# A hybrid decoder step: expert loop reordered, normalisation sums in array groups, z projection threaded through the samples' state update

## The reference

```
h = rmsnorm(x, norm_mix_w) * (1 + sc1) + sh1
qkv, z, b, a, cq, ckv, kpe, gate_a, gate_b = split(h @ w_in)
# gated DeltaNet: 8 heads, DK = DV = 128
q, k = l2norm(q) * DK**-0.5, l2norm(k)                 # per head
# a sample's state S (8 samples x 8 heads x 128 x 128), one step:
S  = S * exp(g);  vn = beta * (v - k @ S);  S = S + outer(k, vn);  o = q @ S
o  = rmsnorm(o, gdn_norm_w) * silu(z)                  # per head, all tokens
# latent attention follows (cq, ckv, kpe ...), then the gates, w_out, and
# mixture of experts: top 4 of 32, for each expert e
gu = xb @ w_gu[e] + b_gu[e]                            # 1024 x 2048
gt, up = min(gu[:, :1024], 7), clip(gu[:, 1024:], -7, 7)
y  = ((up + 1) * gt * sigmoid(1.702 * gt)) @ w_dn[e] + b_dn[e]
out[token] += gate * y
```

## Time and profile before

| | us |
|---|---|
| median of 3 runs | 1761.97 (1761.94 to 1762.75) |
| profiled execution, its own time | 1762.21 |
| its span, first to last instruction | 1760.4 |

### The profile page before, as it was taken

The page is one execution under the profiler, slowest core; times in us unless marked ns, Lnnn a source line. Parts: engine busy times, 40 slices in busy tenths (PEclk is TensorE's granted clock), DMA queues, the critical chain, the costliest instruction groups (busy, mean ns, idle before and its releaser), DMA issues.

```text
span 1760.4 us, 25682 instructions
## 1 busy us (share of the span) xinstructions
PE 1630.7 (93%) x10122; PEld 892.3 (51%) x10122; DVE 495.6 (28%) x1067; ACT 319.1 (18%) x690; POOL 24.2 (1%) x18
## 2 busy tenths in 40 slices
PE   6999688799879999789999999999999999999996
PEld 4777676477547668533343434343433434343433
DVE  1555765511220102422212222222222122222223
ACT  2222121102221110211111211111111112111113
POOL 0000300000000000000000000000000000000000
PEclk8998899899979999879999999999999999999998
DMA  9638312434327986249999999999999999999990
GB/s 405 251 143 338 152 50 109 167 105 139 130 70 272 353 329 292 99 173 394 419 409 422 410 420 412 419 420 408 421 411 419 410 421 410 420 416 414 421 400 25
DMA packets 59535, 541.26 MB, mean 307 GB/s; under 512 B 7218, under 2 KB 11442, under 8 KB 28626
## 3 DMA queue, kind: packets, MB, share of 16 engines
q1 hardware_dynamic: 58754, 534.65, 74.9%
q0 software_dynamic: 720, 5.76, 0.8%
HBM read 533.54 MB, written 6.84 MB: 307 GB/s over the span
## 4 chain that ended last, share of the span: by engine, by line
PE 88%; DVE 7%; ACT 2%; DMA 1%; issue 1%; SPq 0%; POOL 0%; DVEq 0%; ACTq 0%
PE banks L507 25%; PE banks L548 13%; PE banks L1138 8%; PE banks L774 5%; PE banks L463 4%; PE banks L490 4%; PE banks L537 3%; PE banks L477 2%; PE banks L520 2%; PE banks L986 2%; PE banks L1011 2%; DMA ring<-wpre 1%; DVE regB L601 1%; PE banks L1036 1%; PE banks L727 1%; PE banks L872 1%
## 5 line engine op out<-in xcount | busy, mean ns | idle before, releaser
L507 PE MATMUL banks<-ring,regA 128*64 128x512 f32 x2048 | 454.5, 596 | 0.8 <-ACT regA L563 0.8
L507 PEld LDWEIGHTS banks<-ring,regA 128*64 128x64 f32 x2048 | 144.8, 137 | 287.5 <-issue 287.5
L548 PE MATMUL banks<-ring,regC 128*64 128x512 f32 x1024 | 226.8, 595 | 0.0
L601 DVE TENSOR_TENSOR regB<-regB,banks 128x528 f32<-128x528 f32 x132 | 87.0, 700 | 406.0 <-PE banks L490 406.0
L548 PEld LDWEIGHTS banks<-ring,regC 128*64 128x64 f32 x1024 | 70.7, 137 | 131.8 <-issue 127.9
L621 DVE TENSOR_SCALAR regA<-banks 128x512 f32<-128x512 f32 x32 | 22.1, 692 | 344.1 <-PE banks L520 344.1
L566 ACT ACTIVATE regA<-regA 128x512 f32<-128x512 f32 x32 | 20.1, 629 | 531.4 <-DVE regA L621 531.4
L463 PE MATMUL banks<-regC,regA 128*64 128x512 f32 (+1 forms) x396 | 99.7, 622 | 3.2 <-DVE regA L593 3.2
L490 PE MATMUL banks<-regA,regC 64*128 64x264 f32 x528 | 82.2, 422 | 12.6 <-DVE regB L601 11.9
L774 PE MATMUL banks<-hT,ring 128*128 128x264 f32 x384 | 90.3, 391 | 0.0
L774 PEld LDWEIGHTS banks<-hT,ring 128*128 128x128 f32 x384 | 71.5, 190 | 18.2 <-issue 6.8
(11 more groups left out here) (444 smaller groups left out, 1670.6 us busy)
## 6 DMA issues: line engine op xcount, KB each, us to landing
ring<-w_gu SPq DMA_DIRECT2D x128, 2048.0 KB, 10.6
ring<-w_dn SPq DMA_DIRECT2D x64, 2048.0 KB, 8.2
ring<-wpre SPq DMA_DIRECT2D x41, 2048.0 KB, 13.5
ring<-kvT SPq DMA_DIRECT2D x64, 256.0 KB, 4.6
ring<-kv SPq DMA_DIRECT2D x64, 256.0 KB, 6.3
ring<-ssm SPq DMA_DIRECT2D x2, 2048.0 KB, 10.7
o_ssms<-ring POOLq DMA_DIRECT2D x2, 2048.0 KB, 9.4
con_sb<-con SPq DMA_DIRECT2D x1, 1269.0 KB
```

Source lines behind the costliest of these rows:

```text
L507: mm = pe_mm(bank[x // 2][SLOT * (x % 2):SLOT * (x % 2 + 1), :], lhsT=hg[:, k % 4, SLOT * (k // 4):SLOT * (k // 4 + 1)], rhs=ring[c][:, 20 ...
L548: mm = pe_mm(bank[5][SLOT * y:SLOT * (y + 1), :], lhsT=actT[:, m % 4, SLOT * (m // 4):SLOT * (m // 4 + 1)], rhs=ring[c][:, D * (m % 4) + H ...
L601: V.tensor_tensor(pair, pair, banks[:, b:b + 2, 0:T], ALU.add).then_inc(acc_added, 1)
```

## The change

Three edits, made together.

1. **Expert loop.** The scatter's four steps use bank pairs 6-7, 2-3, 4-5, 6-7, and only step 3 waits, for addition 0. The turns of the activation come before the turn of the gathered tokens instead of after it (on ACT too), and the second pair of them waits for the copy of the gathered tokens out of bank 2. `act_` is written by DVE with its columns regrouped (each column 512 bytes from the one before), and the turns read 128 columns side by side.
2. **Row and column groups for the q/k norm and the output norm.** The sums of head i go to partitions 32 (i mod 4) on, with one-hot matrices of 4 (or 2) columns; root and reciprocal run over 128 partitions; the spreads take 4 (or 2) rows in the row group i mod 4. The decay's sums move from behind the 16 spreads to before spread 12.
3. **State update and z projection.** `krow` loses its zeros and each outer product runs over the 32 rows of its head. There are eight steps of two heads, into banks 0-1 and 2-3 in turn; DVE adds each in an operation of 1,024 elements per partition. `project_z` 0 runs before the first step, 1 and 2 are cut into quarters that stand between the eight steps, 3 and 4 follow the two state products, 5 the turns, 6 and 7 the norm's sums. They use banks 6 and 7 and keep all eight results in SBUF (`zs`). The eight spreads run in one go after projection 7, and DVE's multiplications of the heads with them.

```diff
+        SCATTER_BANKS = (6, 2, 4, 6)
...
-                    b = (6, 2)[q % 2]
-                    if q >= 2:
-                        pe.wait_ge(acc_added, j * 4 + q)
+                    b = SCATTER_BANKS[q]
+                    if q == 3:
+                        pe.wait_ge(acc_added, j * 4 + 2)
...
-                turn_gathered(j + 2)
                 pe.wait_ge(act_ready, j + 1)
                 for y in range(2):
+                    if y == 1:
+                        pe.wait_ge(gtok_copied, j + 2)
                     for q in (2 * y, 2 * y + 1):
-                        mm = pe_mm(bank[4 - 2 * y][:, P * q:P * (q + 1)], lhsT=act_[:, q::4], rhs=ident, start=True, stop=True)
+                        mm = pe_mm(bank[4 - 2 * y][:, P * q:P * (q + 1)], lhsT=act_[:, P * q:P * (q + 1)], rhs=ident, start=True, stop=True)
                     mm.then_inc(a_turned, 1)
+                turn_gathered(j + 2)
...
-                V.tensor_tensor(act_[:, :], upc[:, :], sgm[:, :], ALU.mult).then_inc(act_ready, 1)
+                V.tensor_tensor(act_[:, :].rearrange("p (q n) -> p n q", q=4), upc[:, :].rearrange("p (n q) -> p n q", q=4),
+                                sgm[:, :].rearrange("p (n q) -> p n q", q=4), ALU.mult).then_inc(act_ready, 1)
...
+            def group_sum(i, cols):
+                return bank[5][32 * (i % 4):32 * (i % 4) + 4, cols]
...
-                    pe_mm(bank[5][0:2 * H, 0:NPR], lhsT=row_sum(i), rhs=sqb[:, i % 2, 0:NPR], start=(i == 0), stop=(i == 2 * H - 1),
+                    pe_mm(group_sum(i, slice(0, NPR)), lhsT=row_sum(i // 4, 4), rhs=sqb[:, i % 2, 0:NPR], start=(i < 4), stop=(i >= 2 * H - 4),
...
+            def spread(i):
+                if i >= 4:
+                    pe.wait_ge(l2done, i - 3)
+                r = slice(32 * (i % 4), 32 * (i % 4) + 4)
+                pe_mm(bank[L2_BANKS[i % 4]][:, 0:T], lhsT=ident[r, 32 * (i % 4) + i // 4:32 * (i % 4) + i // 4 + 1].to_broadcast([4, P]),
+                      rhs=rsb[r, 0, :], start=True, stop=True).then_inc(l2ss, 1)
...
+                if i == 2 * H - 4:
+                    pe.wait_ge(bg_done, 1)
...
+                spread(i)
...
+            def project_z(m, first, last):
+                if first == 0:
+                    weights(pe, ZZ + m // 4)
+                    if m == 1:
+                        pe.wait_ge(stage("vnm_ready"), 1)
+                    if m >= 2:
+                        pe.wait_ge(stage("z_evac"), m - 1)
+                for k in range(first, last):
+                    mm = pe_mm(bank[7 - m % 2][:, 0:T], lhsT=chunk_k(ZZ + m // 4, m % 4, k), rhs=hT[:, k, :], start=(k == 0), stop=(k == KD - 1))
+                if last == KD:
+                    mm.then_inc(stage("z_ready"), 1)
+            def outer_product(g, x):
+                u = 4 * g + x
+                if x == 0:
+                    pe.wait_ge(stage("vnm_ready"), g + 1)
+                if u >= 2:
+                    pe.wait_ge(stage("snew"), u - 1)
+                for j in (2 * (x % 2), 2 * (x % 2) + 1):
+                    r = slice(32 * j, 32 * j + 32)
+                    mm = pe_mm(bank[j][:, :], lhsT=krow[r, g, :], rhs=vnm[r, g, 512 * (x // 2):512 * (x // 2) + 512], start=True, stop=True)
+                mm.then_inc(stage("outer"), 1)
+            project_z(0, 0, KD)
             pe.wait_ge(*once("krow_copied"))
             for g in range(2):
+                for x in range(4):
+                    outer_product(g, x)
+                    project_z(1 + g, 2 * x, 2 * x + 2)
             for g in range(2):
-                pe.wait_ge(stage("snew"), 3 + g)
-                mm = state_product(0, g, 2 * g)
+                pe.wait_ge(stage("snew"), 4 * g + 4)
+                state_product(0, g, 4 - 4 * g).then_inc(stage("oss_ready"), 1)
+                project_z(3 + g, 0, KD)
...
+            project_z(5, 0, KD)
             pe.wait_ge(stage("on_sq"), 1)
             for h in range(H):
+                mm = pe_mm(bank[3][32 * (h % 4):32 * (h % 4) + 2, 0:T], lhsT=row_sum(h // 4, 2), rhs=oM[:, h, :], start=(h < 4), stop=(h >= 4),
...
+            project_z(6, 0, KD)
+            project_z(7, 0, KD)
             pe.wait_ge(stage("on_root"), 1)
             for h in range(H):
+                if h >= 4:
+                    pe.wait_ge(stage("on_rs"), h - 3)
...
+            pe.wait_ge(stage("z_evac"), H)
...
+                if m % 4 == 2:
+                    pe.wait_ge(stage("on_rs"), H)
...
-            nc.gpsimd.memset(krow[:, :, :, :], 0.0).then_inc(once("krow_zero")[0], 1)
```

More of the change, by code:

```diff
@@ L273, in build_program @@
         stmp = cut(regC, 3700, NSA * P)
[L274 removed]
+        zs = cut(regC, 6600, H, T)
         rot = cut(regC, 8000, T)
@@ L570, in item @@
                 A(selT[:, :], bank[6][:, 0:T], ACT.Copy).then_inc(selT_copied, 1)
-                act.wait_ge(g_turned, j + 2)
-                A(hg[:, :, :], bank[3][:, :].rearrange("p (q s) -> p q s", q=4), ACT.Copy).then_inc(hg_ready, 1)
                 for y in range(2):
@@ L576, in item @@
                       ACT.Copy).then_inc(actT_ready, 1)
+                act.wait_ge(g_turned, j + 2)
+                A(hg[:, :, :], bank[3][:, :].rearrange("p (q s) -> p q s", q=4), ACT.Copy).then_inc(hg_ready, 1)
                 act.wait_ge(moe_read, j * 6 + 6)
@@ L810, in _ @@
-            pe.wait_ge(bg_done, 1)
-            for c in range(2):
-                pe_mm(bank[6][:, 64 + 16 * c:72 + 16 * c], lhsT=upto, rhs=g_tok[:, c, :], start=True, stop=True)
-                pe_mm(bank[6][:, 72 + 16 * c:80 + 16 * c], lhsT=ones, rhs=g_tok[:, c, :], start=True, stop=True)
-            pe.wait_ge(stage("bgm_ready"), 1)
-            mm = pe_mm(bank[6][:, 96:160], lhsT=ones[0:NSA, :], rhs=bgm[0:NSA, :], start=True, stop=True)
-            mm.then_inc(once("cum_ready")[0], 1)
+                if i == 2 * H - 4:
+                    pe.wait_ge(bg_done, 1)
+                    for c in range(2):
+                        pe_mm(bank[6][:, 64 + 16 * c:72 + 16 * c], lhsT=upto, rhs=g_tok[:, c, :], start=True, stop=True)
+                        pe_mm(bank[6][:, 72 + 16 * c:80 + 16 * c], lhsT=ones, rhs=g_tok[:, c, :], start=True, stop=True)
+                    pe.wait_ge(stage("bgm_ready"), 1)
+                    pe_mm(bank[6][:, 96:160], lhsT=ones[0:NSA, :], rhs=bgm[0:NSA, :], start=True, stop=True).then_inc(once("cum_ready")[0], 1)
@@ L960, in _ @@
+            project_z(0, 0, KD)
             pe.wait_ge(*once("krow_copied"))
             for g in range(2):
-                for y in range(2):
-                    u = 2 * g + y
-                    if u < 2:
-                        pe.wait_ge(stage("vnm_ready"), u + 1)
-                    else:
-                        pe.wait_ge(stage("snew"), u - 1)
-                    for j in range(4):
-                        mm = pe_mm(bank[4 * y + j][:, :], lhsT=krow[:, j, g, :], rhs=vnm[:, g, 512 * y:512 * y + 512], start=True, stop=True)
-                    mm.then_inc(stage("outer"), 1)
+                for x in range(4):
+                    outer_product(g, x)
+                    project_z(1 + g, 2 * x, 2 * x + 2)
@@ L979, in _ @@
             mm.then_inc(once("oss_turned")[0], 1)
-            def project_z(m):
-                weights(pe, ZZ + m // 4)
-                if m >= 4:
-                    pe.wait_ge(stage("z_evac"), m - 3)
-                for k in range(KD):
-                    mm = pe_mm(bank[m % 4][:, 0:T], lhsT=chunk_k(ZZ + m // 4, m % 4, k), rhs=hT[:, k, :], start=(k == 0), stop=(k == KD - 1))
-                mm.then_inc(stage("z_ready"), 1)
-            project_z(0)
+            project_z(5, 0, KD)
             pe.wait_ge(stage("on_sq"), 1)
@@ L1005, in _ @@
+                r = slice(32 * (h % 4), 32 * (h % 4) + 2)
+                pe_mm(bank[(0, 1, 4, 5)[h % 4]][:, 0:T], lhsT=ident[r, 32 * (h % 4) + h // 4:32 * (h % 4) + h // 4 + 1].to_broadcast([2, P]),
+                      rhs=ors[r, :], start=True, stop=True).then_inc(stage("on_spread"), 1)
+            pe.wait_ge(stage("z_evac"), H)
             for m in range(8):
@@ L1581, in _ @@
             link(V.memset(gsc[:, :, :, :], 0.0))
-            V.memset(rsb[:, :, :], 0.0).then_inc(once("upad_zero")[0], 1)
+            link(V.memset(rsb[:, :, :], 0.0))
+            V.memset(bank[5][:, 0:T], 0.0).then_inc(once("upad_zero")[0], 1)
             def mod_bias(i, b, at=0):
@@ L1633, in _ @@
                     dve.wait_ge(root_ready, 2)
-                    V.reciprocal(rsb[0:2 * H, 0, :], rsb[0:2 * H, 0, :]).then_inc(stage("l2_rs"), 1)
+                    V.reciprocal(rsb[:, 0, :], rsb[:, 0, :]).then_inc(stage("l2_rs"), 1)
             for i in range(2 * H):
@@ L1776, in _, with gate_z @@
                                 own, ALU.mult).then_inc(stage("vnm_ready"), 1)
-            for u in range(4):
-                g, y = u // 2, u % 2
-                dve.wait_ge(stage("outer"), u + 1)
-                S = ssm_view[g][:, :, 4 * y:4 * y + 4, :].rearrange("p h b v -> p h (b v)")
```

(14 more changed lines are left out.)

75 lines of the change are left out of this document (30 added, 45 removed).

## The result

| | before | after |
|---|---|---|
| median of 4 runs, us | 1762.36 (1761.94 to 1765.77) | 1712.99 (1708.31 to 1715.87) |
| ratio | | 0.9713, 95% interval 0.9688 to 0.9739 |
| profiled execution, own time | 1762.21 | 1711.98 |
| span | 1760.4 | 1710.1 |

A forecast was written before the change was run, and what follows sets the result against it. PE's issue order was taken to bound the kernel, with DMA close behind in the expert loop. Savings of 31.4 + 3.6 + 18.5 = 53.5 us off 1762.2 gave 1708.7, as a median 1708.5 us; range 1694 to 1727.

The forecast's parts named there:

- Edit 1, the scatter: Expert loop: step 3 waits for addition 0 alone and starts when step 2 did, saving 0.61 us an item.
- Edit 1, the turns: Expert loop: activation turned first and read side by side, -0.72, plus 0.35 for the strided write: -0.37 us an item.
- the open term: Expert loop: extra time of DVE's strided write of `act_`, taken as 0.35 us an item, bounds 0 to 0.7.
- Rival A: Expert loop: the strided write is free, the loop gains 42.5 us, total 1697.5 us; chance 28%.
- Rival C: Expert loop: the scattered write competes with PE's reads and incoming loads, making the kernel slower, 1771 us; chance 2%.
- The loop's sum: Expert loop: 32 items save 31.4 us together; DMA caps the gain at about 43 and takes nothing below that.
- The check that I proposed: Expert loop: waits of PE for ring loads in the last items would mean that the DMA binds.
- Rival D: Expert loop: DMA is already busy 100%, so the edits there do nothing, total 1740 us; chance 4%.
- Edit 2: q/k norm: spreads overlap in four row groups and DVE sets the pace, -3.6 us, bounds 0 to -5.
- Edit 3: State update, z projection and output norm: 20.0 us less, -18.5 after the clock charge; bounds -21 and -11.
- clock charge of 1.5: Projection of cq: 1.5 us charged because PE has little to do just before and may drop to half clock.
- Rival B: Eight state steps: 1.2 GHz adds 14 us, 1722.5; or 32-row groups don't overlap, +6.9; both forms together 17%.

The follow-up runs named there:

- experiment 8: Changed kernel with the scatter's old banks (6, 2, 6, 2) and a wait before each of the last two quarters restored: 1728.57 us, ratio 0.9846.
- experiment 6: Kernel of experiment 4 with `act_` written in natural order and the column regrouping left out, so the routed sum is wrongly ordered: 1702.23 us, ratio 0.9674.
- experiment 7: Changed kernel with `act_` written contiguous and its turns reading every fourth column again, as before: 1727.51 us, ratio 0.981.
- experiment 9: Kernel of experiment 5 with the gathered tokens' turns again ahead of the activation's, strided write and contiguous read kept: 1701.31 us, ratio 0.9661.
- experiment 1: Kernel before with only the expert-loop edit (scatter and turns): 1735.52 us, ratio 0.9856.
- experiment 4: Changed kernel with each item's biases loaded ahead of the two w_dn chunks instead of behind all six chunks: 1709.95 us, ratio 0.9725.
- experiment 2: Kernel before with only the q/k norm's row and column groups and the decay's sums before spread 12: 1760.14 us, ratio 0.9993.
- experiment 11: Kernel before with only the decay's sums moved ahead of the 13th of 16 spreads, no row groups: 1762.08 us, ratio 1.0002.
- experiment 10: Kernel of experiment 5 with k in zeroed rows and each outer product of the eight steps over all 128 rows: 1709.57 us, ratio 0.9702.
- experiment 3: Kernel before with only the state update, z projection and output norm changed: 1740.56 us, ratio 0.9888; its profiled execution took 1760.41 us.
- experiment 5: Changed kernel with the biases loaded ahead of w_dn and the last z projection between the spreads of heads 0-3 and 4-7: 1706.15 us, ratio 0.9703.

## Why the prediction was right, and where it was not

**Edit 1, the scatter: right.** -0.61 predicted; taking it back costs 0.61 (experiment 8).

**Edit 1, the turns: right in size, in part by luck.** -0.37 predicted, -0.36 measured (30.30 - 0.61 - 29.33). Experiments 6 and 7 split it: contiguous weights -0.98, the strided write +0.36, and the new order, which uncovers the wait for the product, +0.25 (29.94 in experiment 7 against 30.30 - 0.61 = 29.69). My terms were -0.77, +0.35 and +0.05. The weights' saving was too small by 0.21, because I took it from the chain's times and not from start to start, and the charge for the order was too small by 0.20, so the two cancel. My own times already gave more than 0.05: 1212.65 + 2 x 1.09 is 1214.83 against 1215.41, at most 0.58 earlier and not 0.72. The write was the open term; from the cost of a strided read I took 0.35, and it is 1.05 - 0.69 = 0.36. Rival A is out: the write is not free. By the Trainium skill (page "SBUF — State Buffer", section "Door 1: The DMA port swizzle") every access to a new line of 16 bytes pays; this trace agrees for writes as well, at 0.70 ns an element. The pattern of the write also has short runs of four elements, and no run changes the distance alone; against the runs as the cause speaks that the read L1764, with runs of eight, pays 0.68. Rival C needed 2.0 us and more and is out.

**The loop's sum: the step that failed.** I wrote that "the DMA caps the loop's gain at about 43 us and takes nothing below that". Both halves were off. An item's loads need 29.70 us, not 29.2: in the landings of the chunks four come 4.89 us apart and two 5.06, once the queue never runs dry; my 431 GB/s came from 20 us alone, over 300 us it is 427. With that pace the cap is not 43 us: the loop gained 33.0 us in experiment 6 and 33.2 in experiment 9, and there the chunks' own lead (the time from landing to use) ran out after 19 and 17 items. And in the kernel after the lead that decides is not that of the chunks, 14 to 15.5 us, but the shortest in the item, that of the biases, which SP issues last and for which I had read no row. A deficit of 29.70 - 29.33 = 0.37 us an item used it up by item 16, so I estimate it at about 6 us (7 in experiment 1, with 19 items). From there the loop ran at the pace of the loads: -24.5 us in 31 periods where 30.1 were due. Experiments 1 and 4 show it: it is there without the other edits, and it goes when the biases' load is issued earlier. The check that I proposed named waits for ring loads; the wait came on another load.

The second rule of the Trainium skill that I weighed (page "DMA: Bandwidth & Descriptors", section "Where 436 GB/s comes from", some 358 GB/s per core) would have made the loop unable to gain; the loop moves 427 GB/s. Rival D fell with it, and experiment 1 alone gains 25 us.

**Edit 2: right in kind, the forecast a little too large.** -3.6 predicted. By its own stretch it is -2.7 in the kernel after (14.3 to 11.6, where the first eight instructions took 1.26 us) and -3.3 in experiment 2, where they took 0.73; by the place on the time axis -4.4, of which the rest is an earlier arrival. DVE sets the pace, as I said, but the gap ahead of spread 12, where I had put 1.2 us, is 2.19 in both kernels (in the line of L1661 above), which is most of what is missing. That the sums stand earlier is worth nothing by itself (experiment 11).

**Edit 3: right.** Steps of 2.13 us predicted, 2.15 measured; a clock charge of 1.5 where it cost 2.1; -18.5 predicted, and with the charge -18.2 measured (the 25.2 us by which cq starts earlier, less the 4.9 by which DVE's first operation of the stage was earlier, less 2.1). That the outer products pair in their row groups is shown by experiment 10, though it is worth 0.67 a step and not 0.86, and 0.46 after the changes of shape that it brings.

**The total came closer than its terms.** By their own stretches the edits gave 24.5, 2.7 and 18.2 us, 45.4 of the 53.5 predicted; the spans differ by 50.3. The other 4.9 us are nobody's forecast: 1.7 by which this execution reached the spreads earlier, 2.0 behind the last L629, and 1.2 in between. The time behind the last L629 varies from 31.1 to 34.2 us over the kernels with edit 1 (33.3 or 33.4 in those without it), so that part was at least partly luck.

**Rival B, the clock: real, but not the usual case.** I gave it 17%. It happens in single executions: one is profiled at half clock through the steps (experiment 3), and four others are 15 to 19 us longer than the rest of their kernel's, with the same low mean clock and unprofiled, so for them it is inferred. Its size in the steps is 8 x 1.92 = 15 us; I had 14. What decides it in an execution stays open.

## What to carry to other kernels

When a loop comes near the pace of its loads, price every load in it by its own lead, the smallest ones and the last issued above all; the deficit per item times the items says when each lead is gone, and moving one small issue forward gave back 5.5 us. Where an edit exchanges a strided read for a strided write, put the pair of costs beside each other and then look at what covers each: the write cost 0.36 us where PE waited for it and nothing where the turns of the gathered tokens covered it. Compare two executions from a common point and not by the time axis: the place of cq hid two of the 3.3 us that experiment 5 gained. Subtract starts, not durations, when matmuls are pipelined.

## What the runs showed of the hardware that I had not expected

- **A strided write on VectorE costs what a strided read does.** 512 float32 a partition at a distance of 512 bytes: 1.05 us instead of 0.69, in 32 of 32 instructions (0.70 ns an element, where the read paid 0.68).
- **The same stretch runs at either clock.** With the same 1.9 us pause ahead of them, the eight steps ran at 2.4 GHz (2.15 us each) in the kernel after and at 1.2 GHz (4.07 us each) in the profiled execution of experiment 3, with PE busy all the way in both. By a mean clock of 0.955 to 0.958, 5 of 48 executions were such ones; only one of the five is profiled.
- **Filling a pause is worth more than its length.** With 3.6 us of projection moved into the spreads' waits the next projection started 3.3 us earlier, the clock stayed at 1.00, and its last matmul started 5.8 us earlier.
- **Landings at full load have two paces.** 4.89 us per 2 MB chunk, and 5.06 for two of every six; what lengthens the two is open.
